# Prompt attention: the output products of a head pair's two halves issued together, in turns, with four buffers for the transposed probabilities

## The reference, cut to what matters

```
def cmp_attention(q, kc, vc, q_pos):
    ...
    p = jnp.where(valid, jax.nn.softmax(jnp.where(valid, s, NEG_INF), axis=-1), 0.0)
    o = jnp.einsum("bgjtn,bngd->btgjd", p.astype(vc.dtype), vc).reshape(b, t, NSA_HEADS, NSA_DH)
def selected_attention(q, ks, vs, q_pos, k_pos, blk_ok):
    ...
    p = jax.nn.softmax(s, axis=-1).reshape(b, NSA_KV, NSA_GROUP, t, kk, bl)
    o = jnp.einsum("bgjtkl,bgtkld->btgjd", p.astype(vs.dtype), vs)
def window_attention(q, k, v, q_pos, k_pos):
    ...
    o = jnp.einsum("bgjts,bsgd->btgjd", p.astype(v.dtype), v)
def nsa_merge(o_cmp, o_slc, o_win, g, w_out):
    o = g[:, :, 0, :, None] * o_cmp + g[:, :, 1, :, None] * o_slc + g[:, :, 2, :, None] * o_win
```

## Time and profile before

| | us |
|---|---|
| median of 3 runs (lowest, highest) | 2212.5 (2201.85, 2213.11) |
| the profiled execution's own time | 2199.83 |
| its span in the trace | 2197.9 |
| prompt attention, from the first `s` to the copy of the last round's bank 7 | 280.33 |

### The profile page before, as it was taken

One profiled execution on the slowest core, in us unless ns is written; L12 is line 12 of the kernel. 1 busy time (PEld: TensorE's weight loads), 2 busy tenths in 40 slices (PEclk: granted clock), 3 DMA queues, 4 the chain that ended last, 5 costly groups with the idle time before them and its releaser, 6 DMA issues. The chain is left out here.

```text
span 2197.9 us, 36533 instructions
## 1 busy us (share of the span) xinstructions
PE 2017.8 (92%) x12902; PEld 1684.3 (77%) x12902; DVE 885.0 (40%) x1535; ACT 637.6 (29%) x1209; POOL 327.7 (15%) x582
## 2 busy tenths in 40 slices
PE   8996797999999979989999999989998799999995
PEld 8995586999999879966667444444436789999995
DVE  3225555445432342256666130303032454444323
ACT  3221214333321142355554121212012253333112
POOL 0006110000000000100000433434341100000000
PEclk9998788999999989989999999999999999999998
DMA  6221021222232322400000564747452222222220
GB/s 250 88 92 31 6 96 42 86 86 86 86 93 87 93 77 86 149 1 1 0 0 1 154 213 135 233 131 228 138 196 97 67 63 93 87 86 87 87 79 41
DMA packets 85827, 206.05 MB, mean 94 GB/s; under 512 B 13242, under 2 KB 46555, under 8 KB 84835
## 3 DMA queue, kind: packets, MB, share of 16 engines
q1 hardware_dynamic: 66242, 138.57, 20.2%
q0 software_dynamic: 18336, 58.96, 8.3%
q10 hardware_dynamic: 1152, 7.38, 0.8%
HBM read 188.10 MB, written 16.76 MB: 93 GB/s over the span
## 5 line engine op out<-in xcount | busy, mean ns | idle before, releaser
L1138 PE MATMUL ps<-x_parts,piece_parts 128*128 128x272 f32 x6528 | 829.5, 290 | 36.7 <-DVE x_parts L1624 28.9
L1138 PEld LDWEIGHTS ps<-x_parts,piece_parts 128*128 128x128 f32 x6528 | 825.3, 190 | 41.4 <-issue 24.0
L1467 DVE TENSOR_TENSOR piece_parts<-ring,piece_parts 128x1024 fp32r<-128x1024 f32 (+1 forms) x200 | 241.0, 1205 | 655.1 <-ACT piece_parts L1318 655.1
L1318 ACT ACTIVATE piece_parts<-ring 128x1024 fp32r<-128x1024 f32 (+1 forms) x200 | 208.7, 1043 | 642.7 <-PE ps L1138 612.7
L1138 PE MATMUL ps<-big_parts,piece_parts 128*128 128x272 f32 x2176 | 334.3, 290 | 8.2 <-DVE big_parts L1012 6.6
L1138 PEld LDWEIGHTS ps<-big_parts,piece_parts 128*128 128x128 f32 x2176 | 297.8, 191 | 9.2 <-issue 6.8
L606 PE MATMUL ps<-slots,big 128*128 128x512 f32 x512 | 228.3, 606 | 1.5 <-POOLq L1034 1.4
L606 PEld LDWEIGHTS ps<-slots,big 128*128 128x128 f32 x512 | 98.4, 194 | 123.4 <-issue 121.6
L1138 PE MATMUL ps<-hidden_parts,piece_parts 128*128 128x272 f32 x704 | 145.1, 288 | 0.0
L1138 PEld LDWEIGHTS ps<-hidden_parts,piece_parts 128*128 128x128 f32 x704 | 110.6, 188 | 0.0
L930 DVE TENSOR_TENSOR big<-ps,big 128x508 f32<-128x508 f32 x16 | 11.0, 687 | 205.4 <-ACT big L794 205.4
(11 more groups left out here) (288 smaller groups left out, 2084.8 us busy)
## 6 DMA issues: line engine op xcount, KB each, us to landing
ring<-in_w_up SPq DMA_DIRECT2D x88, 512.0 KB, 3.5
ring<-in_w_in SPq DMA_DIRECT2D x48, 512.0 KB, 3.5
ring<-in_w_down SPq DMA_DIRECT2D x32, 512.0 KB, 3.5
slots<-in_cmp_k SPq DMA_DIRECT2D x128, 128.0 KB, 2.4
slots<-in_cmp_v POOLq DMA_DIRECT2D x128, 128.0 KB, 2.8
slots<-in_slc_k SPq DMA_DIRECT2D x128, 128.0 KB, 2.9
slots<-in_slc_v POOLq DMA_DIRECT2D x128, 128.0 KB, 2.5
ring<-in_w_out SPq DMA_DIRECT2D x16, 512.0 KB, 3.5
```

Of the source, the lines that this page charges most:

```text
L1138: mm = pe.matmul(ps[:, 2 * psum_set + h, 0:HT], split[:, slot % 2, w_part, k * 128:(k + 1) * 128], rhs(k)[v_part][:, h * HT:(h + 1) * HT], ...
L1318: act.activation(split[:, s % 2, 0, 0:size], raw[s][:, 0:size], ACT.Copy).then_inc(w_hi, 1)
L1467: ve.tensor_tensor(split[:, s % 2, 1, 0:size], raw[s][:, 0:size], as_f32(split[:, s % 2, 0, 0:size]), ALU.subtract).then_inc(w_lo, 1)
```

## The change

`o` is called once for a pair of units (u, u+1), at u = 0, 2, 4, 6. It waits for the transposed probabilities of both, and the products of the two halves take turns: for each branch and key block first half 0, then half 1. The calls stand two units later than half 0's stood: after `t(2)`, `t(4)`, `t(6)`, and after `t(7)` for the last pair. `pt_b` has four buffers, of which one lies in the ring's memory, and `ta` and `c` wait for `o(u-4)`. `LEAD["o"]` goes from 2 to 4, which offsets that semaphore's count.

```
-        pt_b = [pt_p, span(F, SLOTS_AT + 2 * 4096 + 512, 9 * 128).rearrange("p (t n) -> p t n", t=9)]
+        pt_b = [pt_p] + [span(F, SLOTS_AT + 2 * 4096 + 512 + k * 1152, 1152).rearrange("p (t n) -> p t n", t=9) for k in range(2)]
+        pt_b.append(span(F, RING_AT + 4320, 1152).rearrange("p (t n) -> p t n", t=9))
...
             def o(R, u, gp):
...
-                UN.done(pe, "ta", R, u)
-                UN.done(pe, "tb", R, u)
-                pt = pt_b[u % 2]
-                for kt in range(qt + 1):
-                    pe.matmul(out, v_nat_p[:, 0, kt, vc], pt[:, kt, :], start=kt == 0, stop=False)
-                for kt in range(qt + 1):
-                    pe.matmul(out, v_nat_p[:, 1, kt, vc], pt[:, 4 + kt, :], start=False, stop=False)
-                pe.matmul(out, vcc_p[0:31, vc], pt[0:31, 8, :], start=False, stop=True).then_inc(UN.sem["o"], 1)
+                UN.done(pe, "ta", R, u + 1)
+                UN.done(pe, "tb", R, u + 1)
+                for v in range(2):
+                    for kt in range(qt + 1):
+                        for g2 in range(2):
+                            pe.matmul(out[g2], v_nat_p[:, v, kt, vc[g2]], pt_b[(u + g2) % 4][:, 4 * v + kt, :],
+                                      start=v + kt == 0, stop=False)
+                for g2 in range(2):
+                    pe.matmul(out[g2], vcc_p[0:31, vc[g2]], pt_b[(u + g2) % 4][0:31, 8, :],
+                              start=False, stop=True).then_inc(UN.sem["o"], 1)
...
                         t(R, u, end)
-                        if u:
-                            o(R, u - 1, gp)
-                    o(R, 7, gp)
+                        if u in (2, 4, 6):
+                            o(R, u - 2, gp)
+                    o(R, 6, gp)
...
-                UN.done(act, "o", R, u - 2)
+                UN.done(act, "o", R, u - 4)
...
-                UN.done(ve, "o", R, u - 2)
+                UN.done(ve, "o", R, u - 4)
```

More of the change, by code:

```diff
@@ L346, in build @@
         pt_p = alloc(9 * 128, e).rearrange("p (t n) -> p t n", t=9)
-        pt_b = [pt_p, span(F, SLOTS_AT + 2 * 4096 + 512, 9 * 128).rearrange("p (t n) -> p t n", t=9)]
-        prob_c = span(F, SLOTS_AT + 2 * 4096 + 512 + 9 * 128, 128).rearrange("p (u n) -> p u n", u=4)
+        pt_b = [pt_p] + [span(F, SLOTS_AT + 2 * 4096 + 512 + k * 1152, 1152).rearrange("p (t n) -> p t n", t=9) for k in range(2)]
+        pt_b.append(span(F, RING_AT + 4320, 1152).rearrange("p (t n) -> p t n", t=9))
+        prob_c = span(F, SLOTS_AT + 2 * 4096 + 512 + 2 * 1152, 128).rearrange("p (u n) -> p u n", u=4)
         bs_p, hid_p = pt_p[:, 0, :].rearrange("p (g n) -> p g n", g=4), pt_p[:, 1, :].rearrange("p (g n) -> p g n", g=4)
@@ L389, in build @@
         QT = (3,3,0,0,2,2,1,1)
-        LEAD = {"o": 2, "t": 1, "ta": 1, "tb": 1}
+        LEAD = {"o": 4, "t": 1, "ta": 1, "tb": 1}
         class Units:
@@ L557, in o @@
             def o(R, u, gp):
-                qt, g2 = QT[u], u % 2
-                out = ps[64 * g2:64 * g2 + 64, 7, qt * 128:(qt + 1) * 128]
-                vc = slice(gp * 128 + g2 * 64, gp * 128 + g2 * 64 + 64)
+                qt = QT[u]
+                out = [ps[64 * g2:64 * g2 + 64, 7, qt * 128:(qt + 1) * 128] for g2 in range(2)]
+                vc = [slice(gp * 128 + g2 * 64, gp * 128 + g2 * 64 + 64) for g2 in range(2)]
                 if u == 0:
                     pe.wait_ge(out_free, R + 1)
-                UN.done(pe, "ta", R, u)
-                UN.done(pe, "tb", R, u)
-                pt = pt_b[u % 2]
-                for kt in range(qt + 1):
-                    pe.matmul(out, v_nat_p[:, 0, kt, vc], pt[:, kt, :], start=kt == 0, stop=False)
-                for kt in range(qt + 1):
-                    pe.matmul(out, v_nat_p[:, 1, kt, vc], pt[:, 4 + kt, :], start=False, stop=False)
-                pe.matmul(out, vcc_p[0:31, vc], pt[0:31, 8, :], start=False, stop=True).then_inc(UN.sem["o"], 1)
+                UN.done(pe, "ta", R, u + 1)
[8 more added lines that the diff above has]
+                              start=False, stop=True).then_inc(UN.sem["o"], 1)
             def two_rounds(i, last):
@@ L757, in ta @@
                 UN.done(act, "t", R, u)
-                UN.done(act, "o", R, u - 2)
+                UN.done(act, "o", R, u - 4)
                 n = (QT[u] + 1) * 128
-                act.activation(pt_b[u % 2][:, 0:8, :].rearrange("p (k t) n -> p k (t n)", k=2)[:, :, 0:n], ps[:, 5:7, 0:n],
+                act.activation(pt_b[u % 4][:, 0:8, :].rearrange("p (k t) n -> p k (t n)", k=2)[:, :, 0:n], ps[:, 5:7, 0:n],
                                ACT.Copy).then_inc(UN.sem["ta"], 1)
@@ L903, in c @@
                 UN.done(ve, "t", R, u)
-                UN.done(ve, "o", R, u - 2)
-                ve.tensor_copy(pt_b[u % 2][0:31, 8, :], ps[0:31, 4, 128:256]).then_inc(UN.sem["tb"], 1)
+                UN.done(ve, "o", R, u - 4)
+                ve.tensor_copy(pt_b[u % 4][0:31, 8, :], ps[0:31, 4, 128:256]).then_inc(UN.sem["tb"], 1)
             def round_(i, gp, last):
```

## The result

The changed kernel takes 2239.76 us in the median of 18 runs (2218.56 to 2264.38), the kernel before 2210.1 in 18 runs (2196.23 to 2219.61). The ratio is 1.0121, interval 1.0094 to 1.0148: 1.2% slower. Forecast were 2181 us, 1.4% faster. The recorded execution took 2261.67 us and is one of the four longest, which are left out of the ratio; the median of the other fourteen is 2236.7. All 18 lose clock: its mean over the whole kernel is 0.899 (the recorded execution) to 0.925 in them, and 0.942 to 0.954 in the runs of the kernel before that stand beside the experiments.

The account below looks back on a forecast made before the run. TensorE's ordered work and waits bound each 33.40 us round. Saving 6.25, less 1.34 and 0.94, gives 3.97; seven rounds give 27.8, the last 3: 31 us off 2212.5, so 2181 us, 8 in 10 from 2162 to 2205.

Parts of the forecast that it names:

- That both halves run at once: Output products on TensorE: a pair costs one half plus 0.02 us, saving 6.25 us a round.
- strict program order: Skill's rule for TensorE matmuls: each pair would last 0.11 us longer, taking 3.5 us off the gain; a trace row disagreed.
- What is given back at the round's end and in the middle: Waits grow where output products move away: 1.34 us before the last pair, 0.94 before t(4), per round.
- The chains of 2.32 and 3.30 us: From s(9)'s end to the last output products, and from t(3) to t(4): both times were to stay.
- The sum at a held clock: Prompt attention stage: 3.97 us saved a round, 31 us together, from 280 to 249 us.
- The clock's term: Half-clock stretches in the stage: eight in eight rounds, 28 us at 1.2 GHz, number kept unchanged.
- The price: Each further low stretch in the stage costs 1.47 us, from a round with one 3.41 us stretch.
- the rivals: One more low stretch per round 0.14, two or more 0.02, half overlap 0.10, no overlap 0.06, nothing given back 0.04.
- two or more per round: Rival: two or more additional low-clock stretches in every round leave a gain of 7 us or less: 2205 us; chance 0.02.

Follow-up runs that it names:

- e12: Changed kernel with each pair's products half after half instead of in turns, and idle products in all four waits of a round; 2217.5 us.
- e2: Changed kernel with idle products ahead of all four waits of a round (before s(3), t(1), t(4) and the last pair); 2168.9 us, ratio 0.9828.
- e4: Kernel before the change, with idle products ahead of its own waits before s(3), t(1) and t(4); 2194.2 us, ratio 0.9950.
- e11: Changed kernel with idle products before s(3), t(1) and t(4), none before the last pair; 2176.4 us, ratio 0.9858.
- e7: Changed kernel with idle products before t(4) and the last pair, none at a round's start; 2197.5 us, ratio 0.9945.
- e8: Changed kernel with each pair's products one unit later and no idle products; 2202.8 us, ratio 0.9955.
- e1: Changed kernel with each pair's products half after half instead of in turns, no idle products; 2317.3 us, ratio 1.0486.

## Why the prediction was wrong

- **That both halves run at once: right.** Pairs of 1.38 and 2.26 us, one half plus 0.02 to 0.04, and 51.6 us between e12 and e2 against 50.0. The sentence that weighed strict program order was decided rightly too: the first passes of both halves start at the same 1115.25.
- **What is given back at the round's end and in the middle: right.** The chains of 2.32 and 3.30 us are in the changed kernel to the hundredth. The waits were forecast at 1.63 and 1.45 us; the trace has 1.55, and 1.22 in two parts.
- **The sum at a held clock: right, on the high side.** e2's stage takes 245 us against the 249 forecast, and its rounds 29.5 us against 29.4. Part of the 245 comes from filling waits that had cost the kernel before its clock; between e4 and e2, both held, the change is worth 25 us by the medians and 28 in the stage, against 31.
- **The clock's term: wrong, and this is the step that failed.** The forecast says of the low stretches "I keep their number as it is for the forecast", and prices any more of them at 1.47 us each. In its place the recorded execution has 266 us at half clock instead of 28. Its stage is 340.61 - 245.18 = 95 us longer than e2's, over 10 us for each of the nine stretches. Filling the waits takes 68 us off the median, more than twice the forecast gain.
- **The price failed more than the number.** The forecast counted eight stretches, from a mean clock and a length of 3.41 us; the trace before has five, and the changed kernel nine. What grew is the length. None of the rivals allowed for that: "two or more per round" is not what happened, and at the constant price even its 2205 us were 35 short.
- **Why the evidence was passed over.** The forecast saw the waits double, from 2.45 to 4.84 us a round, and took its price from one fall, which had o(0) right behind it and followed a stretch with TensorE busy 1.98 of 3.42 us. The fall at 1167.93 of the same trace lasted 10.24 us, three times as long, behind a stretch with TensorE busy 3.01 of 3.41: it lies behind the wait before t(4), the very wait that the change was to lengthen. The forecast does not mention it.
- **What stays open.** What in the work lets the clock come back. That it depends on what stands behind the fall is shown by e11 against the changed kernel: 3.41 us against 13.65 behind the same wait. The longer stretches where o(0) is gone (e7) and where the first pair stands later still (e8) fit this. e1 shows that turns are not needed for the clock to stay down, and e8 that it takes no wait over 1.1 us for it to fall. In the trace before, all five rises lie inside an `o`, and in the changed kernel all nine in a pair or up to 0.11 us behind it; in the filled versions they also lie in transposes and idle products. Which property of these products counts was not tried.

## What to carry to other kernels

Where a change makes TensorE's work shorter and its waits longer, the granted clock is a term of the sum, not a rival: list every low stretch of the trace with its length, price it by what stands behind the place at which the clock falls, and ask whether that is still there after the change. A wait that a chain through other engines sets could here be filled with idle products at a cost of 0.06 us or less, and trying this in the kernel before as well told how much of the gain is the clock's. Two column halves issued in turns ran at the price of one, in accumulations of 3 to 9 products each (one half plus 0.02 to 0.04 us for 2 and 4 key blocks).

## What the runs showed of the hardware

In the changed kernel TensorE is busy 97% of 58 us, with 64-row scores, transposes and products of both halves, and stays at 1.2 GHz. Falls can come at the same place in round after round: in e7 every 34.14 us, six times in a row, with rounds that take 29.5 us in e2, where the clock holds; in e11 every 30.72 us, six times. A fall at one place can last 3.41 or 13.65 us, by what stands behind it (e11 and the changed kernel). Products into the two column halves start in twos: at 1115.25 the first pass of half 1 starts with the first of half 0 and ahead of half 0's second.
